# Heads' squares in two rounded parts, summed on TensorE with a rounded block matrix

## What is computed

```python
def _rmsnorm(x, g):
    xf = x.astype(jnp.float32)
    y = xf * lax.rsqrt(jnp.mean(xf * xf, axis=-1, keepdims=True) + EPS)
    return (y * g.astype(jnp.float32)).astype(x.dtype)

# _shared_kv
s = _rmsnorm(h, g_kv)
k = _rmsnorm((s @ w_k).reshape(n, l, N_KV_HEADS, HEAD_DIM), k_norm)
v = (s @ w_v).reshape(n, l, N_KV_HEADS, HEAD_DIM)
# _window_attention
q = _rmsnorm((xn @ w_q).reshape(n, nb, qb, N_KV_HEADS, Q_PER_KV, HEAD_DIM), q_norm)
```

## Time and profile before

| what | us |
|---|---|
| median of 3 runs | 1399.48 |
| lowest, highest | 1398.52, 1403.1 |
| the profiled execution | 1398.12 |
| its span, first to last instruction | 1396.3 |
| TensorE matmul busy | 1333.8 (96%) |
| GpSimd busy | 782.8 (56%) |
| VectorE busy | 734.1 (53%) |
| ScalarE busy | 445.1 (32%) |

### The profile page before, as it was taken

How to read it: one execution, slowest core, us unless ns; L and a number is a source line. 1 busy time by engine, 2 the same in 40 slices (tenths; PEclk the granted TensorE clock), 3 DMA queues, 4 the chain that set the end, 5 groups by cost and what they waited for, 6 DMA issues and landing times.

```text
span 1396.3 us, 28976 instructions
## 1 busy us (share of the span) xinstructions
PE 1333.8 (96%) x11076; PEld 1295.7 (93%) x11076; DVE 734.1 (53%) x1283; ACT 445.1 (32%) x960; POOL 782.8 (56%) x698
## 2 busy tenths in 40 slices
PE   5688999999999999999999988999999999999998
PEld 4577999999999999999999856999999999999998
DVE  8979233555555541224767775645555555212364
ACT  4753211343334322002242375233434333110021
POOL 4962565566555665555655454645566556555552
PEclk9999999999999999999999999999999999999999
DMA  5034432233332333233553120423223333323232
GB/s 116 1 100 111 110 90 76 78 89 90 90 89 78 88 105 87 85 93 94 124 126 93 46 84 16 102 77 90 79 88 90 90 90 87 104 78 98 79 91 68
DMA packets 226896, 121.20 MB, mean 87 GB/s; under 512 B 23101, under 2 KB 225680, under 8 KB 226364
## 3 DMA queue, kind: packets, MB, share of 16 engines
q1 hardware_dynamic: 216696, 108.04, 27.3%
q10 hardware_dynamic: 10132, 12.20, 3.9%
HBM read 115.18 MB, written 7.07 MB: 88 GB/s over the span
## 4 chain that ended last, share of the span: by engine, by line
PE 87%; DVE 5%; ACT 4%; issue 2%; DMA 1%; ACTq 0%; SPq 0%; DVEq 0%
PE ACC L895 58%; PE MI L895 11%; PE SS L895 9%; PE MI L718 3%; ACT XN L1295 1%; ACT PB L1754 1%; DMA XS<-in_x_prompt_dram 1%; PE SS L1231 1%; PE SS L1109 1%; DVE PB L2345 1%; PE SS L858 1%; DVE RSTD L2130 1%; PE ACC L737 1%; DVE T L2060 0%; DVE T L2054 0%
## 5 line engine op out<-in xcount | busy, mean ns | idle before, releaser
L664 POOL TENSOR_TENSOR SPL<-RAW,SPL 128x1024 fp32r<-128x1024 f32 (+2 forms) x172 | 450.3, 2618 | 14.3
L895 PE MATMUL ACC<-NH,SPL 128*128 128x272 f32 x2016 | 344.4, 289 | 0.7 <-DVE AL L2191 0.7
L661 POOL TENSOR_TENSOR TIC<-EPSB 128x1 f32<-128x1 f32 x172 | 36.8, 214 | 521.4 <-PE ACC L895 340.1
L895 PEld LDWEIGHTS ACC<-NH,SPL 128*128 128x128 f32 x2016 | 287.0, 188 | 1.8 <-issue 0.9
L895 PE MATMUL ACC<-AH,SPL 128*128 128x272 f32 x1408 | 237.6, 289 | 0.0
L895 PE MATMUL ACC<-NL,SPL 128*128 128x272 f32 x1008 | 207.9, 288 | 0.0
L895 PEld LDWEIGHTS ACC<-AH,SPL 128*128 128x128 f32 x1408 | 198.9, 188 | 0.2
L662 POOL TENSOR_SCALAR SPL<-RAW 128x1024 fp32r<-128x1024 f32 (+2 forms) x172 | 196.0, 1140 | 0.2 <-issue 0.2
L895 PEld LDWEIGHTS ACC<-NL,SPL 128*128 128x128 f32 x1008 | 158.4, 188 | 0.0
L895 PE MATMUL ACC<-AL,SPL 128*128 128x272 f32 x704 | 145.3, 287 | 0.0
L1809 DVE SCALAR_TENSOR_TENSOR ACC<-WK,CP,ACC 128x560 f32<-128x560 f32 x88 | 70.9, 805 | 96.9 <-ACT ACC L1295 90.4
(11 more groups left out here) (360 smaller groups left out, 2005.7 us busy)
## 6 DMA issues: line engine op xcount, KB each, us to landing
RAW<-in_w_up_dram SPq DMA_DIRECT2D x88, 512.0 KB
RAW<-in_w_down_dram SPq DMA_DIRECT2D x32, 704.0 KB
RAW<-in_w_glu_dram SPq DMA_DIRECT2D x16, 512.0 KB
RAW<-in_w_ple_gate_dram SPq DMA_DIRECT2D x16, 512.0 KB
KT<-bias_rows SPq DMA_DIRECT2D x64, 64.0 KB, 2.5
RAW<-in_w_q_dram SPq DMA_DIRECT2D x16, 256.0 KB
RAW<-in_w_o_dram SPq DMA_DIRECT2D x32, 128.0 KB
XS<-in_x_prompt_dram ACTq DMA_DIRECT2D x4, 512.0 KB, 11.0
```

The lines of the kernel that those rows point to most:

```text
L661: PIN.tensor_tensor(TIC[:], EPSB[:], EPSB[:], ALU.add)
L664: PIN.tensor_tensor(lo, RAW[:, u, 0:kt, :], hi.bitcast(F32), ALU.subtract).then_inc(sem("split_done"), 1)
L895: last = mm(out[:, h, :], SPL[:, u, w, w0 + k, :], x[:, k0 + k, HT * h:HT * h + HT], start=start and k == 0 and n == 0, stop=stop and k == ...
```

## The change

Two things are done.

1. The squares are kept in two parts. SQ2, a float32r tensor of two rows, is laid over WK's rows 1 and 2. ScalarE makes the square twice, into SQ (fp32) and, rounded, into SQ2's part 0. VectorE's new `square_low(n)` subtracts part 0 from SQ into part 1 and raises `head_low`. BONES becomes float32r. `head_sums` waits for `head_low` and makes four products, two parts by two halves, accumulating, where there were two fp32 products.
2. VectorE's subtractions for the keys' inputs (NL) are made one to a step at s = 0 to 7 where there were two at each of s = 1 to 4, with `square_low(s)` ahead of each.

```diff
-        BONES = perm("BONES", [P, P])
+        BONES = perm("BONES", [P, P], F32R)
...
+        SQ2 = nc.alloc_sbuf_tensor_at("SQ2", [P, 2, NTOK], F32R, offset=wk_at + (WKW * 4 + 31) // 32 * 32)
...
             def head_sums(n):
 
-                pe.wait_ge(sem("head_sq"), n + 1)
-                for h in range(2):
-                    last = mm(SS[:, h, 0:HT], BONES[:], SQ[:, HT * h:HT * h + HT], start=True, stop=True)
+                pe.wait_ge(sem("head_low"), n + 1)
+                for part in range(2):
+                    for h in range(2):
+                        last = mm(SS[:, h, 0:HT], BONES[:], SQ2[:, part, HT * h:HT * h + HT], start=part == 0, stop=part == 1)
                 last.then_inc(sem("head_summed"), 1)
...
                 if n:
                     act.wait_ge(sem("head_summed"), n)
-                A(SQ, src, ACT.Square).then_inc(sem("head_sq"), 1)
+                A(SQ, src, ACT.Square)
+                A(SQ2[:, 0, :], src, ACT.Square).then_inc(sem("head_sq"), 1)
...
+            def square_low(n):
+                dve.wait_ge(sem("head_sq"), n + 1)
+                T(SQ2[:, 1, :], SQ, SQ2[:, 0, :].bitcast(F32), S_).then_inc(sem("head_low"), 1)
+
...
                 evict(s)
                 if s >= 1:
                     head(s - 1)
-                if 1 <= s <= 4:
-                    for m in (2 * s - 2, 2 * s - 1):
-                        low("xq", m, V_GKV, NH, NL)
+                if s <= KC:
+                    square_low(s)
+                if s < KC:
+                    low("xq", s, V_GKV, NH, NL)
                 if s == KC + 1:
                     sample_bias()
...
             evict(KC + 2)
+            square_low(KC + 1)
             maxima(0)
             head(KC + 1)
             evict(KC + 3)
```

More of the change, by code:

```diff
@@ L593, in _ @@
             chain.link(PIN.memset(EPSB[:], EPS))
[L594 to L597, removed]
+            chain.link(PIN.memset(BONES[0:64, 64:128].bitcast(F32), 0.0))
+            chain.link(PIN.memset(BONES[64:128, 0:64].bitcast(F32), 0.0))
+            chain.link(PIN.memset(BONES[0:64, 0:64].bitcast(F32), 1.0))
+            chain.link(PIN.memset(BONES[64:128, 64:128].bitcast(F32), 1.0))
             PIN.memset(TIC[:], 0.0).then_inc(sem("ones_set"), 1)
```

## The result

The changed kernel took 1408.56 us, median of 5 runs (1405.05 to 1410.51), where the kernel before took 1399.48 (5 runs beside it, 1397.87 to 1403.1). The ratio is 1.0057, 95% interval 1.0037 to 1.0077: slower by 0.6%. The profiled execution took 1408.56 with a span of 1406.7, against 1398.12 and 1396.3. The forecast was 1408.0.

What follows compares the result with a forecast made beforehand. TensorE, 96% busy, was taken as the bound, with VectorE's loop close behind. A delay of 6.7 us up to eviction 10 plus 1.8 at the tail made +8.5: 1406.6 profiled, 1408.0 for the median, range 1402.5 to 1411.5.

Steps and rivals of the forecast that it cites:

- the start: Heads 0 and 1: port collisions with GpSimd's copy and subtraction delay eviction 2 from 729.74 to 735.8, +6.1 us.
- the cycles: Evictions 2 to 7: five VectorE cycles of 7.13 us, TensorE's saving waited away, GpSimd waiting instead of VectorE.
- the tail: Last head behind eviction 10: its new subtraction waits for GpSimd's running one, last reciprocal at +6.0 instead of 4.19, +1.8 us.
- eviction 1: VectorE's evacuation of strip 1, forecast to start at 726.3 instead of 721.63, behind GpSimd's subtraction and NL chunk 0.
- eviction 7 to 8: Keys' first strip: TensorE waits for NL chunk 7, putting eviction 8 at 779.8 against 772.66, +7.1 us.
- TensorE's part: Head sums: four rounded products at 0.50 replace two fp32 at 0.92, saving 4.2 us over ten heads if TensorE never waits.
- The reading that would have made this term zero: Head sums: skill text read as an fp32 product costing twice a rounded one, so 0 saved and not 4.2 us.
- Who holds the port: VectorE with two SBUF inputs and GpSimd's splits exclude each other; a waiting 2.27 us GpSimd instruction gets in between VectorE instructions.
- The first rival: Start: VectorE keeps the port at the boundary, eviction 2 at 731.2, +3.9 us in all, 1403.4; chance 0.20.
- Margin: In the cycles, GpSimd's TIC comes inside the new subtraction's hold, 0.36 us after the hold begins, so GpSimd waits.
- Idle time of TensorE: Evictions 2 to 7: TensorE idle 0.6 us ahead of most sums.
- The fourth rival: Start and tail: no collisions at all, +2.5 us, 1402.0, not to be told from no change; chance 0.07.

Runs made afterwards that it cites:

- GpSimd's low part: Changed kernel with heads 1 to 8's low part subtracted on GpSimd, NL subtraction right behind each eviction, heads 0 and 9 summed in fp32; 1395.88 us, ratio 0.9981.
- the repeat: The changed kernel without any edit, run again for a second profiled execution; 1409.11 us, ratio 1.0063.
- squares alone: Changed kernel with the NL subtractions put back in pairs at s = 1 to 4, only the squares' part left; 1412.06 us, ratio 1.0098.
- NL 0 later: Changed kernel with the subtraction for NL chunk 0 moved from s = 0 to s = 1, behind eviction 1 and head 0; 1406.13 us, ratio 1.0054.
- last head fp32: Changed kernel with the last head summed from the fp32 square with fp32 products, without its subtraction; 1408.71 us, ratio 1.0070.
- both ends: Changed kernel with NL chunk 0's subtraction moved behind eviction 1 and the last head summed in fp32; 1402.83 us, ratio 1.0025.
- First and last head in fp32: Changed kernel with first and last heads summed in fp32 from one square, without their subtractions; heads 1 to 8 stay in two parts; 1402.50 us, ratio 1.0012.
- NL 7 early: Changed kernel with the subtraction for NL chunk 7 moved right behind eviction 7; 1408.23 us, ratio 1.0070.
- high part only: Changed kernel with the squares' low part left out: one rounded square, no square subtraction, two rounded products per head; 1395.03 us, ratio 0.9976.

## Why the prediction was right

The sign, the size and the places held: +8.5 forecast, +9.1 in the medians (1408.56 - 1399.48), +9.85 for the second scores on the clock of the profile (806.00 - 796.15). By terms, 8.5 less 0.3 at the start, plus 1.7 in the cycles, less 0.1 at the tail is 9.8. Mechanism and places are the prediction's own; that the median came out only 0.6 from the forecast is in part luck, as the last of the points below says.

| step | forecast | measured |
|---|---|---|
| eviction 1 | 726.3 | 726.15 |
| eviction 2 | 735.8 | 735.50 |
| eviction 4 (2 cycles of 7.13) | 750.06 | 751.49 |
| eviction 7 | 771.45 | 772.91 |
| eviction 7 to 8 | 8.35 | 8.33 |
| eviction 8 to 9, 9 to 10 | 6.5, 7.2 | 6.50, 7.23 |
| eviction 10 to last reciprocal | 6.0 | 5.87 |

- **TensorE's part** held: sums with nothing in front take 0.50 in the chain, 0.42 less than the 0.92 of the earlier trace rows. It is waited away, as said; GpSimd's low part is what cashes it in. The reading that would have made this term zero falls: two fp32 products are not as cheap as four rounded ones.
- **Who holds the port** was an inference from a one-element instruction, and was the term that decides. That a whole subtraction gets in at the boundary held twice in this kernel, 2.91 and 2.85; the 2.20 at the tail has L666 already running, which the rows of before had shown. The first rival, VectorE keeping the port at the boundary, falls with the first of them and with the same 2.92 in the repeat.
- **The start** came 0.3 earlier than worked out (5.76 for 6.1), because the copy had ended a little sooner and the multiply waited 0.07 instead of some 0.5.
- **The cycles** were 7.12 to 7.16 where VectorE bounds them, against 7.13. But evictions 2 to 4 took 15.99 for 14.26, and this is the one term that was missing: behind 4.69 us of idle time TensorE ran at the 1.2 GHz level, strip 3 took 7.83 for 6.03 and came after VectorE was done; behind strip 4, which had the cached keys' transposes in front of it, eviction 4 was still 0.3 late. That is +1.7. The prediction named 4.9 us of idle time and did not ask what it does to the clock.
- **Margin.** The 0.36 us by which GpSimd misses the square's subtraction were put to the test in one cycle of this kernel only, where TIC came 6.32 behind eviction 5 (764.95), at the place forecast, and waited. In the other cycles the strip ended later. It was too slim to rely on: squares alone, NL 0 later, last head fp32 and both ends, which come out of the start otherwise, all missed it, for 0.8 to 2.9 us.
- **Idle time of TensorE** in the cycles was put at 0.6 and reads 0.32 in the timeline (765.20); the restart, 0.1, is not in it. The chain, not this number, shows who bounds.
- **The tail** was put at 1.8, measured 5.87 - 4.19 = 1.68, and given back by the edit that removes it (4.18).
- The median came out at the profiled execution's time and not 1.4 above it as before; that hid part of the missing term. The forecast is closer than its sum, and that is luck: the repeat and the other kernels show that what lies behind the second scores moves by 3 us between executions.

The fourth rival (no collision, all ten heads changed) is none of the kernels run. First and last head in fp32 has no collision either, but its stage is +0.65 where that rival has +2.5; that its median, 1402.50, stands near the 1402.0 worked out is no agreement.

## What to carry to other kernels

Before work is added to the engine beside the bound one, write out both loops to a tenth of a microsecond: a saving on the bound engine counts only down to the next loop's length. An added VectorE instruction with two SBUF inputs costs its own 0.7 us or GpSimd's 2.3, by whether a long GpSimd instruction stands waiting when it is issued, so look at every GpSimd instruction near it, and put it on GpSimd's own list or read one input from PSUM where that can be. Where a new wait leaves TensorE idle for microseconds, count the strip behind it at the lower clock too.

## What the runs showed of the hardware

- A waiting GpSimd instruction gets the port in the gap between two VectorE instructions that follow each other without a pause. Seen with a whole 128x1024 subtraction: 2.91 and 2.92 for 0.78 of work, 4.40 for a pair of 1.47. In the collisions read here the instruction that was issued first went first: L666 at 722.91 ahead of NL at 723.32, L666 at 731.61 ahead of the square's subtraction at 732.02, and the other way round, in NL 0 later, NL at 745.84 (0.78) ahead of the copy at 745.99 (1.54 for 1.05).
- With one input in PSUM the same 128x544 subtraction never waited, 711 to 725 ns in ten of ten.
- The granted clock fell to 0.50 behind TensorE's waits of 4.69 (the change and NL 7 early), 4.68, 4.98 and 2.54 us. Around 2 us it went either way: behind 1.97 it fell once and was kept in seven other executions, behind 2.04 at the tail it fell in NL 7 early and was kept in four others, and behind 1.99, ahead of the second scores, it fell in high part only. The strip behind the long waits then took 7.3 to 8.3 us for 6.03 (7.83, 7.50, 7.33, and 8.28 behind the 2.54), and about 7.0 in squares alone.
- Four rounded 128x272 products take 0.50, two fp32 ones 0.92; behind a wait the four take 0.60.
- A slower TensorE can shorten a stage, when it moves GpSimd's work out of a collision.
